# Start of a gated hybrid layer on one core: x first in SyncE's queue, c from ScalarE's, and the first adaLN tiles split between SyncE's and GpSimd's queues

## What is computed

```
mod = silu(c) @ w_ada + b_ada                  # c: 1 x 4096, w_ada: 4096 x 12288
shift, scale, gate_res = split(mod, 3)
h = rms_norm(x) * norm_w * (1 + scale) + shift   # x: 256 x 4096
proj = h @ w_in                                # q, k, v, z_a, forget logits, x_r, z_r
y_a = (forgetting_attention(q, k, v) * silu(z_a)) @ w_br_attn
y_r = (rg_lru(conv(x_r)) * silu(z_r)) @ w_br_rnn
g_a, g_r = split(sigmoid(h @ w_gate + b_gate), 2)
y = x + gate_res * ((g_a * y_a + g_r * y_r) @ w_out)
```

## Time and profile before

| | |
|---|---|
| median of 3 runs | 2599.47 us |
| the profiled execution | 2599.82 us |
| its span, from the first to the last instruction | 2597.9 us |
| TensorE busy (matmul) | 2556.7 us, 98% of the span |
| VectorE busy | 1908.8 us, 73% |
| ScalarE busy | 1227.8 us, 47% |
| GpSimd busy | 40.0 us, 2% |
| moved by DMA | 700.82 MB, mean 270 GB/s |
| granted TensorE clock, mean | 0.998 of full speed |

### The profile page before, as it was taken

The page is one execution under the profiler, slowest core; times in us unless marked ns, Lnnn a source line. Parts: engine busy times, 40 slices in busy tenths (PEclk is TensorE's granted clock), DMA queues, the critical chain, the costliest instruction groups (busy, mean ns, idle before and its releaser), DMA issues.

```text
span 2597.9 us, 30848 instructions
## 1 busy us (share of the span) xinstructions
PE 2556.7 (98%) x11591; PEld 2124.5 (82%) x11591; DVE 1908.8 (73%) x1885; ACT 1227.8 (47%) x1437; POOL 40.0 (2%) x58
## 2 busy tenths in 40 slices
PE   4999999999999999999999999999999999999999
PEld 4888888888888888888888888888888888888887
DVE  6889999899888666775666666668787878754544
ACT  4554333333333456654665665544444344533333
POOL 0000000000000000220000000000000000000000
PEclk9999999999999999999999999999999999999999
DMA  9999999999998666556666666689898989667675
GB/s 373 368 332 345 329 351 339 338 351 337 349 338 302 175 199 188 160 159 189 198 192 200 197 193 201 198 296 352 312 348 313 348 313 349 213 210 226 210 226 171
DMA packets 353338, 700.82 MB, mean 270 GB/s; under 512 B 26547, under 2 KB 32933, under 8 KB 352933
## 3 DMA queue, kind: packets, MB, share of 16 engines
q1 hardware_dynamic: 352816, 698.74, 80.2%
q10 hardware_dynamic: 372, 0.12, 0.0%
HBM read 694.55 MB, written 4.21 MB: 269 GB/s over the span
## 4 chain that ended last, share of the span: by engine, by line
PE 97%; DMA 2%; DVE 1%; issue 0%; SPq 0%; ACT 0%; DVEq 0%
PE ps_acc L1176 31%; PE ps_acc L1187 31%; PE ps_acc L1178 31%; DMA ada_first<-in_w_ada 1%; PE ps_t L1306 1%; DVE acc L771 0%; PE ps_c L1229 0%; PE ps_t L1260 0%; DMA land<-in_w_gate 0%; PE ps_t L1315 0%; PE ps_t L1253 0%; PE ps_t L1341 0%; PE ps_c L1268 0%; PE ps_t L1238 0%; PE ps_t L1240 0%; PE ps_d L1278 0%
## 5 line engine op out<-in xcount | busy, mean ns | idle before, releaser
L553 ACT ACTIVATE w_hi<-land 128x1024 fp32r<-128x1024 f32 x896 | 949.8, 1061 | 1269.7 <-PE ps_acc L1178 1015.2
L747 DVE TENSOR_TENSOR w_lo<-land,w_hi 128x1024 fp32r<-128x1024 f32 x896 | 1094.0, 1222 | 581.0 <-ACT w_hi L553 578.1
L1176 PE MATMUL ps_acc<-w_hi,h_hi 128*128 128x512 f32 x3060 | 1195.2, 391 | 0.3 <-ACT w_hi L553 0.3
L1178 PE MATMUL ps_acc<-w_hi,h_lo 128*128 128x512 f32 x3060 | 1191.0, 389 | 0.0
L1187 PE MATMUL ps_acc<-w_lo,h_hi 128*128 128x512 f32 x3060 | 818.7, 389 | 0.1
L1187 PEld LDWEIGHTS ps_acc<-w_lo,h_hi 128*128 128x128 f32 x3060 | 573.9, 188 | 121.5 <-DVE w_lo L747 1.8
L1176 PEld LDWEIGHTS ps_acc<-w_hi,h_hi 128*128 128x128 f32 x3060 | 574.5, 188 | 119.3 <-ACT w_hi L553 0.7
L1178 PEld LDWEIGHTS ps_acc<-w_hi,h_lo 128*128 128x128 f32 x3060 | 574.4, 188 | 118.0
L771 DVE SCALAR_TENSOR_TENSOR acc<-ada_ring,cvec,acc 128x1024 f32<-128x1024 f32 x217 | 277.6, 1279 | 8.0 <-DMA ada_ring<-in_w_ada 7.2
L1057 DVE SCALAR_TENSOR_TENSOR racc<-res_land,cvec,racc 128x1024 f32<-128x1024 f32 x124 | 158.6, 1279 | 1.6 <-DMA res_land<-in_w_ada 1.4
L910 DVE TENSOR_TENSOR store<-ps_acc,store 128x1024 f32<-128x1024 f32 x89 | 108.5, 1219 | 11.2 <-PE ps_acc L1187 11.0
(11 more groups left out here) (209 smaller groups left out, 1036.2 us busy)
## 6 DMA issues: line engine op xcount, KB each, us to landing
land<-in_w_in SPq DMA_DIRECT2D x384, 512.0 KB, 4.9
land<-in_w_gate SPq DMA_DIRECT2D x256, 512.0 KB, 4.6
ada_ring<-in_w_ada SPq DMA_DIRECT2D x224, 512.0 KB, 6.0
res_land<-in_w_ada SPq DMA_DIRECT2D x128, 512.0 KB, 7.7
land<-in_w_out SPq DMA_DIRECT2D x128, 512.0 KB, 4.4
land<-in_w_br_attn SPq DMA_DIRECT2D x64, 512.0 KB, 4.4
land<-in_w_br_rnn SPq DMA_DIRECT2D x64, 512.0 KB, 5.8
ada_first<-in_w_ada SPq DMA_DIRECT2D x32, 512.0 KB, 11.6
```

The lines of the kernel that those rows point to most:

```text
L553: act.activation(w_hi[:, n % PARTS], land[:, n % LAND], ACT.Copy).then_inc(hi_rdy, 1)
L747: dve.tensor_tensor(w_lo[:, n % PARTS], land[:, n % LAND], w_hi[:, n % PARTS].bitcast(F32), ALU.subtract).then_inc(split_done, 1)
L1176: pe.matmul(ps_acc[:, par, t], l_hi(kk, t), w_hi[:, n % PARTS, kk], start=first and kk == 0, stop=False)
L1178: ins = pe.matmul(ps_acc[:, par, t], l_lo(kk, t), w_hi[:, n % PARTS, kk], start=False, stop=False)
```

## The change

The transfer of c leaves SyncE's queue and becomes the first in ScalarE's, so that x is the first transfer in SyncE's. The 16 odd tiles of the first adaLN group leave SyncE's queue and are issued by GpSimd, after its constants, with the same waits for their slots as before. The even ones stay where they were, behind x. All lines of the kernel below the first edit shift by 7 (by 6 between the second and the third).

```diff
@@ block.gpsimd, behind the constants
+            for a in range(1, ADA_T, 2):
+                if a - FIRST_SLOTS in FIRST_BY_PE:
+                    pool.wait_ge(ada_by_pe, FIRST_BY_PE.index(a - FIRST_SLOTS) + 1)
+                elif a >= FIRST_SLOTS:
+                    pool.wait_ge(ada_used, ada_done(a - FIRST_SLOTS))
+                pool.dma_start(ada_first[:, a % FIRST_SLOTS], ada_v[:, a, 0:2, 0:CW]
+                               ).then_inc(ada_first_in[a % FIRST_SLOTS], 16)
             pool.wait_ge(ada_used, ada_done(GROUPS * ADA_T - 1))
@@ block.sync
-            sp_.dma_start(cvec[:], c.rearrange("b (p t) -> (b p) t", t=ADA_T)).then_inc(c_in, 16)
             for t in range(NT):
                 sp_.dma_start(x_full[:, t, :], x_v[:, t, :]).then_inc(x_in[t], 16)
-            for a in range(ADA_T):
+            for a in range(0, ADA_T, 2):
                 load_ada(a)
@@ block.scalar
+            act.dma_start(cvec[:], c.rearrange("b (p t) -> (b p) t", t=ADA_T)).then_inc(c_in, 16)
             act.dma_start(raw1[0:64, :], one(b_ada)[0:64, :]).then_inc(small_in, 16)
```

## The result

The changed kernel takes 2608.03 us (median of 9 runs, 2606.73 to 2609.51) where the kernel before takes 2599.65 us (9 runs, 2599.22 to 2601.16). The ratio is 1.0031, with a 95% interval from 1.0022 to 1.0039: 8.4 us slower. The forecast was 2601.8 us within 2598.0 to 2607.5; the time lies above the range.

A forecast was written before the change was run, and what follows sets the result against it. The first 62 us, up to TensorE's first product, were taken to set the end; x's earlier issue and delays to x and tile 0 summed to +2.3 us: 2602.1 us, 2601.8 against the median, range 2598.0 to 2607.5.

The forecast's parts named there:

- What bounds the kernel: Behind 62 us TensorE waits for nothing; whatever moves its first product moves the end by as much.
- x first: x issued at 0.72 us in c's place instead of 1.16: -0.44 us for all that follows in SyncE's queue.
- c from ScalarE: In ScalarE's queue c takes 7.8 us instead of 2.3, covered before VectorE needs the squares: price zero.
- Tile 0 and the pace: VectorE's start on tile 0: 18.27 us, 2.28 late; then a tile pair every 2.71 us, tile 18 at 42.7 us.
- GpSimd's tiles beside x: Odd tiles' packets, taking turns of one packet with x's in the DMA engines, delay x by 1.36 us.
- the first rival: GpSimd's queue gets more than a packet a turn: +6.5 us with two rows, +7.4 with a whole tile; chance 0.24.
- the four chances: Forecast (+0.5 to +4 us) 0.47, first rival 0.24, second 0.08, third 0.21; 0.01 besides for the unseen.
- the sign for the forecast: If right, x's second half lands at 15 to 16 us, seen by the start of ScalarE's second square.
- The tail: Before TensorE's sums: tile 28 at 56.2 us, transposes end at 61.9, VectorE's first half of tile 31 at 61.6: +2.3 us.
- The issues: SyncE has 16 fewer issues; no transfer waited to be issued, so taking them away brings nothing.
- The second rival: GpSimd is slow to issue; at 4 us a tile VectorE waits for odd tiles: +8.6 us, 2608.1; chance 0.08.
- The third: A gain: GpSimd's tiles come once x is through, both queues move more: -0.4 to -3.4 us; chance 0.21.

The follow-up runs named there:

- c and x alone: The kernel before with c first in ScalarE's queue and x first in SyncE's, all 32 tiles staying in SyncE's queue: 2600.01 us.
- the nearest kernel: The changed kernel with c back at the head of SyncE's queue, the odd tiles still issued by GpSimd: 2608.51 us.
- two of three: The changed kernel, but GpSimd issues tiles 0, 1, 3, 4, 6, 7 and so on, SyncE every third one (2, 5, 8 ...): 2600.98 us.
- the run behind x: The changed kernel, but GpSimd waits for the second half of x before its first tile: 2603.83 us.
- the run of eight tiles from ScalarE: The changed kernel, but ScalarE's queue issues the first eight odd tiles, SyncE all from 16 on, GpSimd c and the small inputs: 2602.14 us.

## Why the prediction was wrong

**What bounds the kernel** held. Behind the first product TensorE waits for nothing, and what moved that product moved the end.

**x first** held: -0.44 us in the sum, 0.46 for tile 0 where it was done alone. **c from ScalarE** held as to its price, zero; its sigmoid came at 9.44 us in the change, 7.8 having been reckoned for c. Most of that is not GpSimd's: with c and x alone it came at 8.82.

**Tile 0 and the pace** are the steps that failed, by one size in both: what GpSimd's queue passes in a turn. The text said "I take turns of one packet, because the only two queues that the trace shows side by side took turns like that". The turns are as it says (279 packets against 277). What I did not ask was what a packet is. I counted a packet of GpSimd's as one run of 2 KB, as in SyncE's queue, and it is two runs. So tile 0 has 32 runs of the odd tiles between its own 16, not 16: it came 4.2 us behind x, where the sum had 2.71. Behind it a pair of tiles took 3.9 us instead of 2.71, up to tile 6. Tile 0 was put at 18.27 us and came at 20.03. Of the 6.5 us by which VectorE ended late, 4.0 are tile 0's and 2.5 are longer waits: 5.5 us in all (1.88, 0.76, 1.22, 1.10 and 0.52) instead of 3.0. From tile 10 on VectorE waited for no landing; tile 18, put at 42.7 us by its landing, had its turn at 46.8 (37.07 and seven tiles of 1.39 us) by VectorE's own work, and VectorE's end, put at 62.3, was at 66.67.

**GpSimd's tiles beside x** was put at +1.36 us, and 1.7 were measured (the second half of x landed at 15.8 us, 14.1 with c and x alone). That is near, by luck: two runs a turn would have made it 2.7, as the first rival had it, but GpSimd's packets began some 4 us after the issue that the sum counted from. How much of the difference that makes no run separates.

Two slips in the sums change nothing: 42.7 and 19.4 us make 62.1 and not 62.3, and the four chances with the 0.01 for the unseen make 1.01.

**The first rival** was this mechanism, with its first price: two rows a turn, tile 0 at 21 us, VectorE's end at 66.7. It came out at 20.03 and 66.67. That the end fits to a tenth is luck: tile 0 came 1.0 us sooner, and VectorE waited 5.5 us and not 4.5. I gave it 0.24, and that was too little: the trace showed turns between two queues of one kind, and said nothing about how the third cuts its packets. Its signs, a second square at 17 us or later and tile 0 at 21 or later, were not met (16.37 and 20.03 us), because most of the loss arises behind x. Nor was the sign for the forecast, a second square at 15 to 16 us, and the square was a poor sign: ScalarE was at the first square until 16.28 us, while x had been there since 15.8. The Trainium skill (DMA: Bandwidth & Descriptors, "SWDGE vs HWDGE vs iDMA") says that GpSimd's packets are of 4096 bytes at most by preference, and the 2304 packets of the change agree. The prediction had cited the Trainium skill for another sentence of the same page, with packets of typically 9 to 17 descriptors ("Queues, rings and completion order"). By that the odd tiles would have gone through whole, with tile 0 near 26 us; at 20.03 us and two runs a packet the trace disagrees.

**The tail** failed too, and took the time out of the range. The sum put tile 28 at 56.2 us, the transposes until 61.9 and VectorE's first half of tile 31 at 61.6. But the transposes hang on a landing and the sums on VectorE's additions. As soon as VectorE falls behind the transfers, a gap opens between them: tile 28 landed at 54.79 us, the sums came at 66.07, and TensorE's clock fell between. It was in no rival. In the change it is 1.5 us from VectorE's end to the first product (3.45 against 1.97); tying the transposes to VectorE's use took 2.4 us off the time of the nearest kernel. With it the first rival would have stood at 6.5 + 1.5 = 8.0 us, 2607.5 us, the upper end of the range; the median is 0.5 us above that.

**The issues** held: no gain from the 16 fewer shows. **The second rival** falls: GpSimd issued a tile in 0.72 us. **The third** falls: the rate did not rise.

## What to carry to other kernels

Two busy queues shared the DMA engines packet by packet, so the share of each goes by how large its packets are, and not by how many bytes wait; read the packet counts of the queues before splitting a stream between them. When a consumer takes the pieces in a fixed order, split them so that they land in that order, as two of three did here, or leave them in one queue: where one queue already moved 387 GB/s, the second only changed which piece came first. Count for the second queue from its first packet and not from its issue. And work that is there to keep TensorE's clock up should wait for the same thing as the work that it warms up for.

## What the runs showed of the hardware

GpSimd's queue joins runs into packets of 4 KB, also across partitions: 4 data packets an engine for 256 KB in runs of 2 KB (2560 packets for 32 such transfers). SyncE's and ScalarE's queues made one packet of each run of 2 KB (17 an engine and tile with the completion), and SyncE's one of each of x's 16 KB. Two busy queues passed equal numbers of packets: 1392 and 1392 from 20 to 40 us with two of three tiles from GpSimd. An issue on GpSimd took 0.72 us for 512 KB and 0.54 us for 256 KB, and its first packet came over 4 us after the start of its first issue (2.06 and 6.2 us in the change, 14.45 and 18.8 in the run behind x); what fills that time no run shows. In the run of eight tiles from ScalarE the sixth issue, at 4.19 us, took 8.07 us beside x; of the five before it four took about half a microsecond each and one 1.31. TensorE's granted clock was the surprise: after 8.03 us without work the sums took 3.7 us in the change, at the lower level (1.2 GHz), and after 2.42 us without work 2.2 us in the run of eight tiles from ScalarE, at the full one (2.4 GHz).
